# The expert stage of a hybrid encoder step: transposes moved from TensorE to VectorE, five weight sets instead of four, the down product on four column tiles

## The reference, cut to what matters

```
g_idx = argmax(t @ w_router_group + b)              # one of 4 groups
top_v, top_i = top_k(expert logits of the group, 2) # two of its 8 experts
for e in range(32):
    hid = silu(t @ w_gate[e]) * (t @ w_up[e])       # 1024 -> 256, twice
    out = out + (hid @ w_down[e]) * combine[:, e]   # 256 -> 1024
```

## Time and profile before

| | us |
|---|---|
| median of 3 runs (928.66 to 932.1) | 930.59 |
| the profiled execution | 932.57 |
| its span, first to last instruction | 930.8 |
| first gather issued / first weight reload issued | 594.28 / 606.97 |
| last scatter issued, landed | 896.49, 900.20 |

### The profile page before, as it was taken

The page is one execution under the profiler, slowest core; times in us unless marked ns, Lnnn a source line. Parts: engine busy times, 40 slices in busy tenths (PEclk is TensorE's granted clock), DMA queues, the critical chain, the costliest instruction groups (busy, mean ns, idle before and its releaser), DMA issues. The chain is left out here.

```text
span 930.8 us, 19000 instructions
## 1 busy us (share of the span) xinstructions
PE 864.2 (93%) x8017; PEld 682.8 (73%) x8017; DVE 350.1 (38%) x767; ACT 192.7 (21%) x432; POOL 136.2 (15%) x173
## 2 busy tenths in 40 slices
PE   3999999979999999999999998699999999999945
PEld 2778877867888888877889886576667767676722
DVE  5599896333642122410223456511111111111116
ACT  2312306434221110122221211111111111111103
POOL 1190100002420000000000000112222222222200
PEclk9999999989999999999999998599999999999977
DMA  9630072202121660071002033689999999999536
GB/s 245 212 98 1 5 183 91 91 12 93 47 91 68 226 237 1 1 226 46 1 5 104 29 114 154 251 305 350 336 370 359 369 377 364 386 377 372 228 83 245
DMA packets 71418, 166.48 MB, mean 179 GB/s; under 512 B 20592, under 2 KB 51440, under 8 KB 58496
## 3 DMA queue, kind: packets, MB, share of 16 engines
q1 hardware_dynamic: 58500, 150.86, 45.7%
q0 software_dynamic: 6144, 9.45, 3.1%
q10 hardware_dynamic: 6716, 5.34, 1.8%
HBM read 158.09 MB, written 17.88 MB: 189 GB/s over the span
## 5 line engine op out<-in xcount | busy, mean ns | idle before, releaser
L904 PE MATMUL bank<-act_a,weight_ring 128*128 128x288 f32 x768 | 192.9, 413 | 1.8 <-ACT act_a L1444 1.8
L904 PEld LDWEIGHTS bank<-act_a,weight_ring 128*128 128x128 f32 x768 | 147.8, 194 | 42.6 <-ACT act_a L1444 2.4
L1212 PE MATMUL bank<-weight_ring,act_b 128*128 128x256 f32 x512 | 111.9, 380 | 0.0
L1212 PEld LDWEIGHTS bank<-weight_ring,act_b 128*128 128x128 f32 x512 | 97.0, 190 | 12.7
L1381 PEld LDWEIGHTS bank<-region_t,weight_ring 128*64 128x64 f32 x2048 | 74.1, 142 | 14.3 <-issue 13.5
L1381 PE MATMUL bank<-region_t,weight_ring 128*64 128x80 f32 x2048 | 76.9, 237 | 1.9 <-issue 1.2
L1767 DVE TENSOR_TENSOR region_t<-region_t,bank 128x160 f32<-128x160 f32 (+3 forms) x47 | 15.5, 331 | 132.2 <-PE bank L1381 131.7
L830 POOL DMA_INDIRECT expert_rows<-region_r,scatter_now x32 | 30.1, 940 | 200.2 <-DVE region_r L2269 200.2
L1116 PE MATMUL bank<-weight_ring,region_u 128*128 128x256 f32 x256 | 58.3, 388 | 0.0
L2269 DVE COPY region_r<-bank 80x512 f32<-80x512 f32 x32 | 22.0, 687 | 96.3 <-PE bank L1393 96.3
L1393 PE MATMUL bank<-weight_ring,region_t 128*80 128x512 f32 x128 | 57.6, 593 | 0.0
(11 more groups left out here) (336 smaller groups left out, 1093.4 us busy)
## 6 DMA issues: line engine op xcount, KB each, us to landing
weight_ring<-in_w_gate SPq DMA_DIRECT2D x16, 1024.0 KB, 10.2
weight_ring<-in_w_down SPq DMA_DIRECT2D x16, 1024.0 KB, 12.5
weight_ring<-in_w_up SPq DMA_DIRECT2D x16, 1024.0 KB, 13.2
weight_ring<-in_w_in SPq DMA_DIRECT2D x8, 1024.0 KB, 8.4
region_g<-in_w_gate SPq DMA_DIRECT2D x8, 1024.0 KB, 11.1
region_g<-in_w_up SPq DMA_DIRECT2D x8, 1024.0 KB, 14.4
act_a<-in_w_down SPq DMA_DIRECT2D x8, 1024.0 KB, 13.3
act_a<-in_w_gate SPq DMA_DIRECT2D x8, 1024.0 KB, 11.4
```

Source lines behind the costliest of these rows:

```text
L904: m = pe.matmul(ps[:, 0:HALF], slot(c)[:, k, P * (mt % 2):P * (mt % 2 + 1)], x[:, k, HALF * h:HALF * (h + 1)], start=(k == 0), stop=(k == ...
L1212: m = pe.matmul(ps[0:L, CW * cc:CW * (cc + 1)], x[:, k, t0:t0 + L], slot(c)[:, k, :], start=(k == 0), stop=(k == KD - 1))
```

## The change

- The transposes leave PE. After the gather, VectorE transposes `xg[b]` straight into `xgT[b]` in twelve instructions, each of 32 partitions by 8 squares of 32x32 (four column parts times three row blocks; the rows are padded from 80 to 96). The copies of the transposed rows by ACT and DVE go with them.
- Gate and up of expert n write banks 2b and 2b+1, so banks 0 to 3 are used in pairs by turns.
- The down product is cut into 24 matmuls of at most 32 rows by 256 columns. Row blocks 0, 1, 2 of the first three column quarters go to column tiles 0, 1, 2, and the last quarter of each block to column tile 3.
- A fifth weight set: `WSET` has fifteen buffers, the first loads are issued in a new order as soon as scores and values of the attention have freed their buffers, and a buffer is loaded again for expert n+5.
- PE's first pass is written out for all 32 experts. PE's order is gate and up of n+1, down of n. DVE's order is hidden of n, transposes of n+2, result rows of n-1. POOL's order is gather of n+3, scatter of n.

The core of the diff (left out: constants and buffers' addresses, semaphore names, the loop bounds of PE's and ACT's passes, the second pass):

```diff
+SETS = 5
+        c0, c1, t1 = view(conv, 0, 2048), view(conv, 2048, 2048), view(reg_t, 2048, 2048)
+        WSET = [[t1, ring_k[5], ring_k[0]], [c0, g0, c1], [g1, ring_k[1], ring_k[2]],
+                [ring_k[3], ring_k[4], b0], [b1, a0, a1]]
+        PREFETCH = [(0, 1), (0, 2), (1, 1), (2, 0), (0, 0), (1, 0), (1, 2), (2, 1), (2, 2), (3, 0), (3, 1), (3, 2),
+                    (4, 0), (4, 1), (4, 2)]
...
+            def reload(p, i, n):
+                N = NE * p + SETS * i + n
+                for part in range(3):
+                    if part < 2:
+                        sp.wait_ge(gu_done, N - (SETS - 1))
+                    else:
+                        sp.wait_ge(dn_done, 2 * N - 2 * (SETS - 1))
+                    load_part(SETS * i + n, n % SETS, part)
...
             def pool_pass(p):
...
-                with pool.Fori(1, LAST) as i:
-                    for b in range(2):
-                        gather(first + i + 1, i + 1, b)
-                        scatter(first + i, i, b)
+                for n in range(3):
+                    gather(n, 0, p, reused=n >= 2)
+                for n in range(3):
+                    gather(n + 3, 0, p)
+                    scatter(n, 0, p, reused=again or n >= 2)
+                with pool.Fori(0, (NE - 6) // 2) as i:
+                    for n in range(3, 5):
+                        gather(n + 3, i, p)
+                        scatter(n, i, p)
...
-            def turn_x(pp, b):
-                pe.wait_ge(gathered[b], 16 * pp + 16)
-                for h in range(2):
-                    for k in range(4):
-                        m = turn(banks[h][:, CAP * k:CAP * (k + 1)], xg[b][0:CAP, 4 * h + k::KD])
-                    m.then_inc(turned_x, 1)
...
+            def down_rows(N, n, i, p, reused=True):
+                pe.wait_ge(hid_ready, N + 1)
+                wait_expert_chunk(pe, 2, n, i, p)
+                if reused:
+                    pe.wait_ge(yo_act, N)
+                    pe.wait_ge(yo_dve, N)
+                for r in range(3):
+                    for j in range(2):
+                        for blk, quarter in [(0, r), (1, r), (2, r), (r, 3)]:
+                            m = pe.matmul(down_block(b, blk, quarter), hid[b][:, j, DB * blk:min(CAP, DB * (blk + 1))],
+                                          down[:, D * j + CW * quarter:D * j + CW * (quarter + 1)],
+                                          start=(j == 0), stop=(j == 1))
...
+            def turn_x(n, i, p, reused=True):
+                b = n % 2
+                dve.wait_ge(gathered[b], 16 * (NE // 2) * p + 16 * i + 16 * (n // 2 + 1))
+                if reused:
+                    dve.wait_ge(gu_done, NE * p + 2 * i + (n - 1))
+                for part in range(4):
+                    for blk in range(3):
+                        m = dve.transpose(
+                            xgT[b][DB * part:DB * (part + 1), :, DB * blk:DB * (blk + 1)],
+                            xg[b][DB * blk:DB * (blk + 1), CW * part:CW * (part + 1)].rearrange("p (c k) -> p k c", k=KD))
+                m.then_inc(turned_x, 1)
...
+            def dve_rows(n, i, p, reused=True):
+                dve.wait_ge(dn_done, 2 * NE * p + 4 * i + (2 * n + 2))
+                if reused:
+                    dve.wait_ge(scattered[b], 16 * (NE // 2) * p + 16 * i + 16 * (n // 2))
+                dve.tensor_copy(yo[b][DB * 2:CAP, 3 * CW:D], down_block(b, 2, 3))
+                dve.tensor_copy(yo[b][0:CAP, 2 * CW:3 * CW], banks[5 + 2 * b][0:CAP, 0:CW]).then_inc(yo_dve, 1)
...
+                with dve.Fori(0, (NE - 6) // 2) as i:
+                    for n in range(4, 6):
+                        dve_hidden(n, i, p)
+                        turn_x(n + 2, i, p)
+                        dve_rows(n - 1, i, p)
```

More of the change, by code:

```diff
@@ L46 @@
 CAP = 80
+DB = 32
+XS = 96
 PASSES = -(-T // CAP)
+SETS = 5
+BODY = 10
 SKIP = float(1 << 12)
@@ L418, in build @@
         par_loaded = sem("s5_params_loaded")
-        more_loaded = [sem(f"more_loaded{i}") for i in range(6)]
+        more_loaded = [sem(f"more_loaded{i}") for i in range(3 * SETS)]
         row_loaded = [sem(f"row_loaded{i}") for i in range(3)]
@@ L661, in sp_pass, with load_part @@
[L661 to L667, removed]
+            def load_part(e, s, part):
+                sp.dma_start(WSET[s][part], experts_of[part][bass.ds(e, 1), :, :]
+                             .rearrange("e p n -> p (e n)")).then_inc(WSEM[s][part], 16)
@@ L668, in sp_pass @@
                     for s in range(SETS):
                         for part in range(3):
-                            load_part(first + i, i, s, part)
+                            load_part(s, s, part)
+                whole = NE // SETS - 1
+                with sp.Fori(0, whole) as i:
+                    for s in range(SETS):
+                        reload(p, i, SETS + s)
+                for n in range(SETS * (whole + 1), NE):
+                    reload(p, 0, n)
             def rows_scattered(p):
@@ L1406, in pe_pass @@
                 pe.wait_ge(idx_ready, p + 1)
-                turn_x(2 * first, 0)
-                for s in range(SETS):
-                    expert(first, s, reused=again or s >= 2)
-                with pe.Fori(1, QUADS - 1) as i:
-                    for s in range(SETS):
-                        expert(first + i, s)
-                for s in range(SETS):
-                    expert(first + (QUADS - 1), s, last=(s == SETS - 1))
+                gate_up(N0, 0, 0, p, reused=again)
+                gate_up(N0 + 1, 1, 0, p, reused=again)
+                down_rows(N0, 0, 0, p, reused=again)
+                if not again:
+                    for n in range(2, NE):
+                        gate_up(n, n, 0, p)
+                        down_rows(n - 1, n - 1, 0, p)
+                else:
+                    with pe.Fori(0, (NE - 2) // BODY) as i:
+                        for n in range(2, 2 + BODY):
+                            gate_up(N0 + i * BODY + n, n, i, p)
+                            down_rows(N0 + i * BODY + (n - 1), n - 1, i, p)
+                down_rows(N0 + NE - 1, NE - 1, 0, p)
             pe_pass(0)
@@ L1724, in act_expert @@
                 act.activation(yo[b][0:CAP, 0:512], banks[4 + 2 * b][0:CAP, :], ACT.Copy).then_inc(yo_act, 1)
             def act_pass(p):
-                first = p * (LAST + 1)
                 again = not isinstance(p, int)
-                copy_x(first, 0)
-                for b in range(2):
-                    act_expert(first, b, reused=again)
-                with act.Fori(1, LAST) as i:
-                    for b in range(2):
-                        act_expert(first + i, b)
-                for b in range(2):
-                    act_expert(first + LAST, b, last=(b == 1))
+                act_gate(0, 0, p)
@@ L1738, in _ @@
+                for n in range(1, 4):
+                    act_gate(n, 0, p)
+                    act_rows(n - 1, 0, p, reused=again or n > 2)
+                with act.Fori(0, (NE - 4) // 2) as i:
+                    for n in range(4, 6):
+                        act_gate(n, i, p)
+                        act_rows(n - 1, i, p)
+                act_rows(NE - 1, 0, p)
+            act.sem_inc(yo_act, 1)
             act_pass(0)
```

186 lines of the change are left out of this document (89 added, 97 removed).

## The result

The changed kernel takes 1112.07 us (median of 4 runs, 1110.88 to 1112.99) against 929.62 us for the kernel before (4 runs, 926.93 to 932.10): 1.197 times the time, with an interval of 1.1945 to 1.1994. The forecast was 1050 us, with a range of 985 to 1125. The profiled execution took 1110.88 us, its span is 1109.1 us.

The account below looks back on a forecast made before the run. The prediction took PE and DMA as full before, and a closed chain through DVE and POOL as the new bound: 0.98 + 2.00 + 4.4 + 5.4 + 0.9 = 13.7 us, 28 turns, plus start and tail: 1050 us, range 985 to 1125.

Parts of the forecast that it names:

- The chain closes: Expert stage: rows n-2, scatter n-2, gather n+2, transposes n+2, rows n-1 form a closed chain, 13.7 us per expert.
- scatter and gather at 0.98 and 2.00 us: Chain links on POOL: rows ended to scatter issued 0.98 us, scatter issued to gather issued 2.00 us.
- the ring: The closed chain; in e1 and e6 over two turns: rows n, scatter n, gather n+5, transposes n+5, rows n+2.
- Gather, 4.4 us: Chain link from gather issued to landed: 4.4 us taken, between 3.3 with idle and 8.0 with full DMA engines.
- Transposes, 5.4 us: Chain link on DVE: twelve transposes of an expert, one after another at 0.45 us each, 5.4 us (3.4 to 8.2).
- Rows and steps, 0.9 us: Chain link on DVE: two copies of result rows and the steps between, 0.9 us (0.6 to 1.4).
- The sum: Expert stage: rows of 0 at 621.2 us, then 28 turns of 13.7 us, 383.6 us in all, to 1004.8.
- The tail: After rows of 28 at 1004.8 us: last experts to 1019.3, then an unchanged 30.6 us, to a span of 1049.9.
- the band called likely: Chain at 12.5 to 15.5 us a turn, giving 1016 to 1100 us: 56 in 100.
- Column tiles side by side, 2.6 us: PE's down product: four column tiles run side by side, six rounds of two passes, 2.6 us in place of 3.5.
- The rival on the half clock: PE at half clock needs 14.4 us an expert and sets the pace: 1070 us; PE-pace rival 8 in 100.
- The DMA-bound rival, 914 us: Expert stage: chain does not close, weight loads set the pace at 9.7 us an expert: 914 us; 8 in 100.

Follow-up runs that it names:

- e1: The changed kernel with POOL issuing gather n+4, in place of gather n+3, before scatter n: 952.81 us.
- e2: The changed kernel with each transpose reading its squares contiguously, not with a stride of 8 elements (output not the reference's): 1056.58 us, one run.
- e12: e5 run again (the kernel before with only the down product on four column tiles), on the same chip as e10 and e11: 920.69 us.
- e6: The changed kernel with POOL's gather one expert earlier and normed rows stored permuted, so transposes read runs of 32 elements: 917.38 us.
- e5: The kernel before with only the down product on four column tiles and the small row copies that go with it: 921.81 us.
- e11: e6 run again, on the same chip as e10 and e12: 918.92 us.
- e7: The kernel before with five weight sets, column tiles and experts written out, but PE's transposes and POOL's order as before: 925.02 us.
- e10: e6 with four weight sets and PE's experts 2 to 29 in a loop of four experts a turn: 924.55 us.

## Why the prediction was right, and where its sum was off

- *The chain closes.* Shown: each link is in the trace at the place named, scatter and gather at 0.98 and 2.00 us to the digit, and e1, which changes only the place of the gather in POOL's order and so closes the ring over two turns, takes 159 us away. PE's share fell, the gather is waited for in each expert, weights land in 6.7 us, and the DMA share is 0.60 (0.7 was written).
- *Gather, 4.4 us.* Measured 3.71. The weights' burst is behind it as argued; in e2, with turns of 13.59 us, it is 4.34, so the shorter turn of the forecast explains most of the difference.
- *Transposes, 5.4 us.* The step that was mis-sized: 7.69. The start-to-start time of 0.45 was taken from copies and small operations, none of which reads with a stride of eight elements; such a transpose takes 0.629. The upper end of its range (8.2) held it. e2 measures the same twelve at 5.37 with contiguous reads, so the error is the stride and nothing else.
- *Rows and steps, 0.9 us.* Measured 0.89.
- *The sum.* 28 turns took 430.9 us (631.57 to 1062.42), where 383.6 were written: +47.3. That is about 28 times +2.29 for the transposes and -0.69 for the gather, and 3.5 more in the first turn, of 18.8. The two errors have opposite signs: with the gather right and the transposes as written the forecast would have been 19 us lower. The first rows came at 631.6 instead of 621.2, +10.4, again transposes: the first 24 take 15.51 us where 10.8 were written, and the next two sets of twelve 7.88 and 7.90 where 5.4 were.
- *The tail.* 1109.1 - 1062.4 = 46.7 against 45.1: +1.6, with PE's gate and up at the lower clock. Together 59.3, which is 1109.1 - 1049.9 but for 0.1. So the turn of 15.27 us lies at the edge of the band called likely (12.5 to 15.5), and the time, 1112, above that band's 1100: of the slowdown of 182 us the forecast had 120.

The start and the tail stand in these rows of the timeline, in the form of the earlier trace rows:

```profile
598.52 15.51 DVE L2294 STREAM_TRANSPOSE region_t<-region_r 32x256 f32<-32x256 f32 x24 [0.98 <-DMA region_r<-ffn_rows,gather_index]
...
606.42 4.54 PE L1402 MATMUL bank<-region_t 128*64 128x80 f32 x64 [11.76 <-DVE region_t L2294]
...
1062.00 0.42 DVE L2314 COPY region_r<-bank 80x256 f32<-80x256 f32 x1
...
1075.54 0.92 POOL L861 DMA_INDIRECT expert_rows<-region_r,scatter_now  x1 [1.47 <-DVE region_r L2314]
```

- *Column tiles side by side, 2.6 us.* Measured 2.80 busy, the next product 2.7 later. By itself this part is worth 8 us (e12): 0.7 us a turn until the weights bind.
- *The clock.* The rival on the half clock named the right symptom and the wrong consequence: the granted clock did fall, to 0.78, but not to 0.50, and PE stayed off the chain.
- *The DMA-bound rival, 914 us.* It held that a gather issued one step earlier opens the chain and leaves max(7.2, 9.7) us. e1 and e6 have the gather there, and the chain closes over two turns instead (19.62 and 17.81 us). e6, at 917.38, comes close to the 914 by its number alone: its turn is 8.88 us and PE waits for no weight in it. The price of 9.7 us for an expert's weights is right, as the last turns of e5 and e12 show (9.76 and 9.74).
- *"Writing the experts out costs nothing while PE waits for something else."* True in the changed kernel, whose list of waits shows no such stop on PE between 605 and 890 us, and false as soon as the wait goes: 14.5 us in e6, 8.1 in e11, 12.7 in e7.

Left open: how long a loop may be before its code is fetched again in each turn. Between four experts and ten nothing was tried. Also open is what e6 would take with the ring of two turns cut: no run has a third buffer for gathered rows or the transposes elsewhere in VectorE's order.

## What to carry to other kernels

Where two engines' orders are written by hand, write down for each waiting instruction what stands behind it, and follow the links until they end or close: a gather queued behind a wait for results closed a ring here that left PE, VectorE and the DMA engines idle two fifths of the time. One step in POOL's order gave back 159 us, and it only stretched the ring over two turns: follow the links again after each repair, and don't take a time that comes out as forecast for proof of the reason. Price a data movement by its access pattern and not by its element count, by a run of the pattern if no row has it. Cheaper engine work is worth only what is left until the next bound, here 8 to 12 us until weights or the ring, and code written out to get it has a price of its own that hides behind whatever the engine waits for today.

## What the runs showed of the hardware that was not expected

- A VectorE transpose of 32 partitions by 256 float32 takes 629 ns when it reads every eighth element, 435 ns when it reads runs of 32; of 128 elements, strided, 376 ns.
- PE stops for code. With the DMA engines full, written-out code stops it for about 1 us every second expert (12.2 us in 12 times), a loop of ten experts stops it up to 4.99 us at once and fetches as much as code written out (31 packets against 32), a loop of four fetches next to nothing (1 to 4) and stops it for 2 to 3 us, all before 665 us (kernel before and e10). Each of 97 stops, over all traces, ended 1.21 to 1.81 us after a packet of instructions had come in.
- Full DMA engines fall behind without a sign in the engines' busy times: in e5 gate loads land after 8.8 us around 645 us and 32.4 around 840, with 378 GB/s moved between 760 and 820 us. The four sets hid it from PE until about 805 us. The gather feels it at once: 3.71 us to the transposes at a DMA share of 0.60, 8.60 at 1.00 (e6).
- A scatter that frees a buffer lands late under that load, 7.7 us after its issue in e1 against 3.71 at the end of the kernel before: ACT waited 107.5 us in 17 times for it. It cost nothing there, as the next scatter still started 0.93 us after VectorE's rows.
